# The second norm scale of a SwiGLU block: from the gated product on GpSimd to the down projection's output on VectorE

## The reference

```python
def rms_norm_2(x, g):
    xf = x.astype(jnp.float32)
    y = xf * lax.rsqrt(jnp.mean(xf * xf, axis=-1, keepdims=True) + NORM_EPS)
    return (y * g.astype(jnp.float32)).astype(x.dtype)

def swiglu(h, w_gate_up, w_down):
    g, u = jnp.split(h @ w_gate_up, 2, axis=-1)
    return (jax.nn.silu(g) * u) @ w_down

x = x + swiglu(rms_norm_2(x, ffn_norm[l]), w_gate_up[l], w_down[l])
```

## Time and profile before

| | |
|---|---|
| median of 3 runs | 1871.3 us (1869.64 to 1872.98) |
| span of the profiled execution | 1868.3 us |
| TensorE busy | 1848.6 us, 99% |
| VectorE busy | 1121.4 us, 60% |
| ScalarE busy | 785.5 us, 42% |
| GpSimd busy | 281.0 us, 15%, 216 instructions |
| TensorE's granted clock | 1.00 of full speed in the whole span |

### The profile page before, as it was taken

How to read it: one execution, slowest core, us unless ns; L and a number is a source line. 1 busy time by engine, 2 the same in 40 slices (tenths; PEclk the granted TensorE clock), 3 DMA queues, 4 the chain that set the end, 5 groups by cost and what they waited for, 6 DMA issues and landing times.

```text
span 1868.3 us, 24067 instructions
## 1 busy us (share of the span) xinstructions
PE 1848.6 (99%) x9096; PEld 1479.3 (79%) x9096; DVE 1121.4 (60%) x1974; ACT 785.5 (42%) x1728; POOL 281.0 (15%) x216
## 2 busy tenths in 40 slices
PE   8999999999999999999999999999999999999999
PEld 6887777888888888776678888888877788888887
DVE  7455896754454466588875535445978765445343
ACT  6445876332232232376643323223468533233221
POOL 2000552211010111111021101101210121011010
PEclk9999999999999999999999999999999999999999
DMA  6221000223233223322122333322342222323323
GB/s 232 69 92 67 24 1 24 93 100 101 92 101 92 100 86 107 101 79 75 52 94 98 93 99 102 91 102 81 106 119 63 65 100 90 102 92 100 98 89 96
DMA packets 51538, 166.57 MB, mean 89 GB/s; under 512 B 6880, under 2 KB 7264, under 8 KB 51168
## 3 DMA queue, kind: packets, MB, share of 16 engines
q1 hardware_dynamic: 51424, 165.03, 27.4%
HBM read 155.05 MB, written 2.10 MB: 84 GB/s over the span
## 4 chain that ended last, share of the span: by engine, by line
PE 93%; DVE 4%; ACT 1%; issue 1%; DMA 0%; SPq 0%; POOL 0%; DVEq 0%; ACTq 0%
PE bank L987 25%; PE bank L989 25%; PE bank L988 25%; PE bank L1096 2%; PE bank L1145 2%; PE bank L961 2%; PE bank L963 2%; PE bank L962 2%; PE bank L1010 1%; PE bank L1223 1%; DVE WL L1601 1%; PE bank L1175 1%; PE bank L1187 1%; PE bank L1120 1%; PE bank L1200 1%
## 5 line engine op out<-in xcount | busy, mean ns | idle before, releaser
L1290 ACT ACTIVATE WH<-RAW 128x512 fp32r<-128x512 f32 (+2 forms) x584 | 331.5, 612 | 757.1 <-PE bank L989 682.7
L1601 DVE TENSOR_TENSOR WL<-RAW,WH 128x512 fp32r<-128x512 f32 (+2 forms) x584 | 463.7, 829 | 64.0 <-ACT WH L1290 58.2
L987 PE MATMUL bank<-GH,WH 128*128 128x512 f32 x1088 | 433.8, 399 | 0.9 <-DVE SM L1818 0.7
L987 PE MATMUL bank<-HH,WH 128*128 128x512 f32 x1056 | 423.4, 401 | 3.2 <-DVE HL L1616 1.4
L989 PE MATMUL bank<-GH,WL 128*128 128x512 f32 x1088 | 424.1, 390 | 0.0
L988 PE MATMUL bank<-GL,WH 128*128 128x512 f32 x1088 | 423.6, 389 | 0.0
L989 PE MATMUL bank<-HH,WL 128*128 128x512 f32 x1056 | 411.7, 390 | 0.0
L988 PE MATMUL bank<-HL,WH 128*128 128x512 f32 x1056 | 411.4, 390 | 0.0
L2157 POOL TENSOR_TENSOR TMP<-TMP,RST 128x512 f32<-128x512 f32 x66 | 116.8, 1770 | 863.9 <-DVE TMP L2072 863.9
L987 PEld LDWEIGHTS bank<-GH,WH 128*128 128x128 f32 x1088 | 204.4, 188 | 49.2 <-issue 7.3
L987 PEld LDWEIGHTS bank<-HH,WH 128*128 128x128 f32 x1056 | 198.3, 188 | 53.7 <-issue 8.3
(11 more groups left out here) (246 smaller groups left out, 1860.8 us busy)
## 6 DMA issues: line engine op xcount, KB each, us to landing
RAW<-in_wgu SPq DMA_DIRECT2D x132, 512.0 KB, 3.2
RAW<-in_wd SPq DMA_DIRECT2D x48, 512.0 KB, 3.5
RAW<-in_wd SPq DMA_DIRECT2D x24, 384.0 KB, 3.2
RAW<-in_da_qk SPq DMA_DIRECT2D x16, 512.0 KB, 3.3
TMP<-TMP SPq DMA_DIRECT2D x104, 64.0 KB, 2.0
RAW<-in_w_inh SPq DMA_DIRECT2D x12, 512.0 KB, 3.3
RAW<-in_w_out SPq DMA_DIRECT2D x8, 512.0 KB, 3.7
RAW<-in_da_v SPq DMA_DIRECT2D x8, 512.0 KB, 3.2
```

Source lines behind the costliest of these rows:

```text
L987: e.matmul(b, w_h, hi[st.x][k], start=(k == 0), stop=False)
L1290: e.activation(whs[s % NW][:, a:b], raw[s % NR][:, a:b], ACT.Copy).then_inc(S["wh"], 1)
L1601: e.tensor_tensor(wls[s % NR][:, a:b], raw[s % NR][:, a:b], whs[s % NW][:, a:b].bitcast(F), ALU.subtract).then_inc(S["wl"], 1)
```

## The change

GpSimd's multiply of the gated product by `RST` is taken out. The product goes to ScalarE's split as it is, the down projection works on it unscaled, and since the scale belongs to a token and so to a column of the output tile, each of the eight outputs of every down part is multiplied by `RST` on VectorE, from PSUM into `TMP` 4 or 5, before the addition to `xt[m]`. The wait `settle` between the two lets the first finish. The planner gets 1400 instead of 620 ns for that step. Two dependences are added to the steps of the value projections: the last contraction step of token block 0 of `hv` and `dv1` comes after the last unit of the stage before, and a unit's first four steps, one for each token block, come each after the last step of the same token block of the unit before.

```diff
@@ plan: dense, stages with per
                           operand(name, k), k == 0 and bank_before(name, i), u > 0 and t == 4 * st.per - 1 and last[u - 1],
+                          k == 7 and i == 0 and name in ("hv", "dv1") and last[st.u0 - 1],
+                          ul > 0 and t < 4 and ("tri", name, u - 1, 4 * (st.per - 1) + t),
                           kind=("tri", u), first=0 if early else 4 + u, take=take if k == 0 and i == 3 else None)
@@ plan: residual
-            o.add("DVE", ("resv", name, m), 620, of(name, m), kind="ff")
+            o.add("DVE", ("resv", name, m), 1400 if name[0] == "f" else 620, of(name, m), kind="ff")
@@ plan: ffn
-                o.add("POOL", ("e_gug", f, kk), 1300, ("e_guv", f, part, 2 * k + 1))
-                o.add("ACT", ("fhia", f, kk), 520, ("e_gug", f, kk), last[ST[free].u0 + ST[free].n - 1])
+                o.add("ACT", ("fhia", f, kk), 520, ("e_guv", f, part, 2 * k + 1), last[ST[free].u0 + ST[free].n - 1])
@@ scalar: ff_high
-                p.wait_ge(S["ff_y"], g + 1)
+                p.wait_ge(S["ff_o"], FF[f] + ST[f"{f}g{part}"].m0 + 2 * k + 2)
@@ vector: res
                 p.wait_ge(S["unit"], unit_of(st, m))
+                if st[0] == "f":
+                    p.then(e.tensor_tensor(tmp[4 + m % 2], b, RST[:, :], ALU.mult))
+                    p.settle()
+                    b = tmp[4 + m % 2]
                 e.tensor_tensor(xt[m], b, xt[m], ALU.add).then_inc(S[sem], 1)
@@ gpsimd
-            def ff_scale(f, kk):
-                g, (part, k) = FA[f] + kk, part_of(kk)
-                s = tmp[g % 4]
-                p.wait_ge(S["ff_o"], FF[f] + ST[f"{f}g{part}"].m0 + 2 * k + 2)
-                e.tensor_tensor(s, s, RST[:, :], ALU.mult).then_inc(S["ff_y"], 1)
```

More of the change, by code:

```diff
@@ L648 @@
     "a_chain v_chain g_chain wh wl unit tm_p "
-    "st_sq st_acc lz_a lz_e2 lz_pe lz_rst lz_ln lz_c oph op ff_o ff_up ff_y ff_hi ff_act "
+    "st_sq st_acc lz_a lz_e2 lz_pe lz_rst lz_ln lz_c oph op ff_o ff_up ff_hi ff_act "
     "in_o vg_o hv_o h3_o h3_t h3_v wo_o dv_o qk_o do_o ks_o vs_o sq_o so_o "
@@ L2151, in nad @@
                 e.tensor_tensor(o_, o_, nt[kb % 2], ALU.add).then_inc(S["n_om"], 1)
-            def ff_scale(f, kk):
-                g, (part, k) = FA[f] + kk, part_of(kk)
-                s = tmp[g % 4]
-                p.wait_ge(S["ff_o"], FF[f] + ST[f"{f}g{part}"].m0 + 2 * k + 2)
-                e.tensor_tensor(s, s, RST[:, :], ALU.mult).then_inc(S["ff_y"], 1)
             steps = {"pag": accumulate, "zerosg": consts, "cs": cs, "decg": dec, "dech": dec_queries,
-                     "eqmg": wh0, "nad": nad, "e_gug": ff_scale}
+                     "eqmg": wh0, "nad": nad}
             for name, *at in PLAN:
```

## The result

The changed kernel is slower: median 1881.7 us (1878.13 to 1883.56, four runs) against 1870.5 us (1869.49 to 1872.98, four runs) for the kernel before, a ratio of 1.0054 with an interval of 1.0040 to 1.0069. The forecast was 1877.0 us, slower, with a range up to 1882.5: right in direction and inside the range, but the cost was forecast at 5.7 us and came out at 11.2 in the first comparison and 8.4 in the second.

A forecast was written before the change was run, and what follows sets the result against it. TensorE was taken as the bound, busy 1848.6 of 1868.3 us. Stalls of 3.5 and 1.5 us plus 0.7 at the end sum to 5.7, added to 1871.3: 1877.0 us, slower, range 1869.0 to 1882.5.

The forecast's parts named there:

- What leaves GpSimd and VectorE: 66 GpSimd multiplies, 116.8 us, and up to 72 us of VectorE work go, worth 0 us at the end.
- The pair's price: Each of 72 residuals becomes multiply then addition, starting 0.73 us apart, costing VectorE 0.72 us more each.
- The period: Third down parts of blocks 1 and 2: each VectorE period adds 0.47 us of lag with 512-column splits, 0.35 with 384.
- Rival (b): VectorE's collision with GpSimd stays whole in the third down parts: period 4.8 us, stalls 8.1, 1879.4 us; chance 0.19.
- The lag: VectorE runs 2.5 us late at the last residual of the third down parts; bounds 0 and 5.0.
- The wait at `dv0`: Block 1 into the value projection: TensorE waits 3.5 us for the last residual, 1.0 even without lag.
- The wait at `ks`: Block 2 into the shared key projection: TensorE stalls 1.5 us on the sum of squares, last operand right behind.
- The end: Program end: the last residual's longer step delays the last store by 0.73 us, with no cover.
- The early value projections: Their products move under the dependences, none is added, TensorE is full: 0 us, bound 2 us either way.
- Rival (c): Faster: the attention chain starts up to 8 us earlier, shrinking 5.4 us idle at 200 to 320 us; 1867.6 us; chance 0.12.
- 3.0 us between span and median: Profiled span 1868.3 us, median 1871.3; the difference was put down to what lies around the span.
- new order: The whole order is planned anew and the mixer stretch depends on it: a bound of 2 us either way.

The follow-up runs named there:

- one_ahead: The changed kernel, but the second added dependence leaves out one step, so one value-projection block may run ahead of block 1's last residual: 1878.76 us, ratio 1.0043.
- deps_only: The kernel before with the two planner dependences alone, scaling still on GpSimd: 1871.83 us, ratio 1.0009.
- no_meeting: The changed kernel, but GpSimd sums squares of 8 instead of 512 columns in the third parts of blocks 1 and 2: 1871.94 us, ratio 1.0007.
- third_gpsimd: The changed kernel, but the third down parts keep GpSimd's scaling and the single-addition residual: 1872.57 us, ratio 1.0014 against the kernel before.
- dose: The changed kernel with the multiply made twice in each residual of the third parts of blocks 1 and 2: 1890.44 us, ratio 1.0103.
- fill_both: The changed kernel with 15 extra matmuls ahead of the value projection's wait and eight ahead of the key projection's: 1878.6 us, run again 1877.8 us.
- fill_one: The changed kernel with 15 extra matmuls ahead of the value projection's wait only: 1880.76 us, ratio 1.0048 against the kernel before.
- plan_true: The changed kernel, only the planner's scaled-operand cost raised from 1500 ns to 2250 (block 1) and 1800 (block 2): 1877.37 us, ratio 1.0031.
- after_again: The changed kernel, unaltered, measured once more (the second comparison): 1879.76 us against 1871.4 us for the kernel before, ratio 1.0048.
- third_vector: The changed kernel, but only the third parts are scaled on VectorE, the first two parts by GpSimd: 1879.96 us, ratio 1.0051 against the kernel before.

## Why the prediction was right or wrong

- **What leaves GpSimd and VectorE.** Right: GpSimd 163.8 us and 150 instructions (forecast 164 and 150), VectorE 1085.9 (about 1100). The mean weight split went from 829 to 703 ns, and by its count of 584 that is 74 us, against the 72 forecast. None of it was on the path.
- **The pair's price.** Right: multiply to addition 0.71 us, forecast 0.73 from the rotary pair.
- **The period.** Right within 0.1 us: periods with splits of 512 columns take 4.63 us (forecast 4.55), those with 384 take 4.38 (4.43). The forecast read the partial give-back well: the square starts 0.04 us behind the addition instead of 0.34, and the low half took 1.67 instead of 1.80. Rival (b), with nothing given back and a period of 4.8, has the nearer price for the second comparison (1879.4 against 1879.76) without being what happened.
- **The lag.** Right: the last multiply of f1 starts at 717.30, the unit's last matmul ends at 714.72, so it is 2.45 us over the 0.13 of a punctual one. The forecast was 2.5.
- **The wait at `dv0`.** Right: 3.36 us, forecast 3.5. `one_ahead` shows that the dependence's own share is one product, 0.66 us, and `deps_only` that with the short residual of before it is 0.18. The 1.0 us forecast for the long residual without a lag is 0.83 in `no_meeting`.
- **The wait at `ks`.** Near in size, wrong in what it waits for. Forecast: 1.5 us on the sum of squares, until E + 6.1, with the last operand right behind at E + 6.65. Measured: E is 1338.46, the wait ends at 1345.18, E + 6.72, on that last operand, 1.97 us; the new plan makes the sum over the squares later, at 1346.67. The operand's time was forecast to 0.1 us.
- **The end.** Right: 0.72 us, forecast 0.73.
- **The early value projections.** Right at 0: from 20 to 700 us TensorE is busy 673.09 us before and 673.10 after. Rival (c), faster by a better start of the attention chain, had nothing in it.
- **The sum.** The three terms measured 6.05 against 5.7. The step that fell short is the one that turned them into a time: "Sum 3.5 + 1.5 + 0.7". It takes a wait of TensorE to cost its own length. Behind the 3.36 us the clock was at half speed and nine matmuls took 1.69 us more than they do at full clock; the other three runs of the first comparison have a mean clock of 0.995 to 0.997, and the median lies 3.6 us above the profiled time. The prediction had the clock's row of the kernel before, 1.00 everywhere, and gave it no term and no rival, although the change brought the first idle stretch of this length into a dense stage.
- **The range and the addends.** That the measured time lies in the range is in part luck: the room above the forecast was kept for a longer lag, and the lag came as forecast, while a low clock that had no term used the room up. The stated upper end of 1882.5 us doesn't follow from the bounds either: 1871.3 + 10.7 is 1882.0, and 1884.0 with the 2 us of new order. And the 3.0 us between span and median are not all around the span: in each run recorded the time is 1.7 to 2.2 us above the same run's span, and the rest is the difference between runs. The forecast difference isn't touched by that, since it was added to the median.

What is shown and what isn't: that the lag makes the waits is shown by `third_gpsimd` and `dose`, and that it needs GpSimd's meeting by `no_meeting`. That the idle stretch at `dv0` brings the low clock there is shown by the windows: it came in all six profiles with a wait of 2.3 us or more and in none of the three with it filled. That the low clock costs some 2 us of the median rests on two comparisons whose intervals overlap. The low clock also came in single executions in other places (200 to 210 us in `fill_both`, 0.83; 1380 to 1390 us in `fill_one`, 0.83), and why some runs have more of it, as most of the changed kernel's do, stays open; of the 11.2 us of the first comparison about 3 are accounted for by no trace. Of the eleven runs with both waits filled four were at 1.000, and of the nine of the changed kernel none.

## What to carry to other kernels

Before work is moved to an engine with spare time, read the busy share of the engine in the window where the moved step falls, not in the whole: VectorE was 60% busy overall and 94 to 99% in the stretches that decided, and there it isn't the step's own length that counts but whether the period around it still closes. A step that adds to an eight-fold chain is paid at the chain's end, by whoever needs the last result. And price a new idle stretch of TensorE above its length: here 3.4 us of idle time cost 1.7 us more in slow matmuls behind it, while 2.0 us cost nothing more in three profiles.

## What the runs showed of the hardware

- **The clock reacts to short idle stretches, but not each time.** Behind 3.36 us of idle time the windows of 2 us read 0.77, 0.50, 0.87 and then 1.00, behind 2.7 us 0.62 and 0.53 (`one_ahead`), behind 2.3 us 0.84, 0.50 and 0.80 (`plan_true`). Behind 2.0 us they stayed at 1.00 in three profiles (the changed kernel, `after_again`, `third_vector`) and fell to 0.50 in two (`one_ahead`, `fill_one`); behind 0.83 us they stayed at 1.00 (`no_meeting`). In `one_ahead` six matmuls behind the wait of 2.7 us still start at close to the full pace before those that are 0.43 us apart. The Trainium skill (TensorE: Matmul & The Clock Gate, Part 1) has the clock go to half speed after idleness; the trace agrees with 0.50.
- **At half clock a matmul of 512 columns starts every 0.43 us** (719.93 to 720.36 in the changed kernel) instead of 0.227, and is shown with 0.63 instead of 0.39.
- **The meeting has about one price in either order.** GpSimd's addition of 128x512 makes the VectorE instruction that meets it 0.9 to 1.1 us longer: the low half (1.63 to 1.82 against 0.75), a pair of splits (2.38 against 1.29) or the gain product (1.50 against 0.48). GpSimd's own addition takes 1.28 to 1.41 us where it starts ahead of the low half, and 1.58 where it starts while the low half runs. Changing which step meets it moved the cost; only the period that had no low half at all was free of it.
